# Moving the weight halves by 64 bytes in the on-chip memory of a decoder-trunk kernel

## The reference, cut to what matters

```python
def swiglu(x, wi, wo):
    gt, up = jnp.split(x @ wi, 2, axis=-1)
    return (jax.nn.silu(gt) * up) @ wo

def trunk(x, p, ssm0, conv0, k_hist, v_hist, pos0, hist_valid, w):
    for i in range(DEPTH):
        x = x + 0.5 * swiglu(rmsnorm(x, w['ffn1_norm'][i]), w['ffn1_wi'][i], w['ffn1_wo'][i])
        h = rmsnorm(x, w['mix_norm'][i])
        ...   # mixer (layer 0) or attention (layer 1): out
        x = x + out
        x = x + 0.5 * swiglu(rmsnorm(x, w['ffn2_norm'][i]), w['ffn2_wi'][i], w['ffn2_wo'][i])
        gate = jax.nn.sigmoid(rmsnorm(x, w['ple_norm'][i]) @ w['ple_gate'][i])
        x = x + gate * (p[i] @ w['ple_proj'][i])
```

## The kernel before, in words

| operand | first tile | step from tile to tile | tiles begin at |
|---|---|---|---|
| xh, xl | 128 | 32 | 128, 160, 192, 224, 0, 32, 64, 96 |
| xh2, xl2 | 64 | 32 | 64, 96, 128, 160, 192, 224, 0, 32 |
| hh, hl | 128 | 32 | 128, 160, 192, 224, 0, 32, 64, 96, then again |
| views of wide | 16 | 0 | always 16 |

## Time and profile before

### The profile page before, as it was taken

How to read it: one execution, slowest core, us unless ns; L and a number is a source line. 1 busy time by engine, 2 the same in 40 slices (tenths; PEclk the granted TensorE clock), 3 DMA queues, 4 the chain that set the end, 5 groups by cost and what they waited for, 6 DMA issues and landing times.

```text
span 1182.9 us, 26670 instructions
## 1 busy us (share of the span) xinstructions
PE 1171.8 (99%) x9823; PEld 1150.3 (97%) x9823; DVE 867.8 (73%) x1378; ACT 699.3 (59%) x1150; POOL 248.1 (21%) x354
## 2 busy tenths in 40 slices
PE   9999999999999999999999999999999999999998
PEld 9999999999999899999999999999999899999998
DVE  8667646999899868787645987888468777677448
ACT  6454435777786647555546765555368765544345
POOL 1000002412222202232344233232036310000001
PEclk9999999999999999999999999999999999999999
DMA  8765554755445375876886677657743346555552
GB/s 311 239 205 187 178 180 142 265 186 206 144 168 194 110 227 195 303 233 246 283 307 209 225 272 277 221 175 245 249 155 98 107 158 214 179 181 189 178 183 86
DMA packets 63345, 239.90 MB, mean 203 GB/s; under 512 B 7716, under 2 KB 9680, under 8 KB 58896
## 3 DMA queue, kind: packets, MB, share of 16 engines
q1 hardware_dynamic: 56880, 197.83, 50.1%
q0 software_dynamic: 6112, 40.66, 9.5%
q10 hardware_dynamic: 288, 0.54, 0.1%
HBM read 226.87 MB, written 13.39 MB: 203 GB/s over the span
## 4 chain that ended last, share of the span: by engine, by line
PE 85%; DVE 8%; ACT 3%; issue 2%; DMA 1%; POOL 1%; SPq 0%; DVEq 0%; POOLq 0%; ACTq 0%
PE bank L520 27%; PE bank L521 27%; PE bank L522 27%; DVE wlo L1596 2%; ACT whi L1111 1%; DVE xact L1871 1%; DVE xl L1615 1%; DMA raw<-weights 1%; PE bank L894 1%; DMA x<-xT 0%; POOL sq L2227 0%; DVE x L1626 0%; PE bank L920 0%; PE bank L899 0%; ACT under L1513 0%
## 5 line engine op out<-in xcount | busy, mean ns | idle before, releaser
L1596 DVE TENSOR_TENSOR wlo<-raw,whi 128x1024 fp32r<-128x1024 f32 x367 | 457.9, 1251 | 240.1 <-ACT whi L1111 239.7
L1111 ACT ACTIVATE whi<-raw 128x1024 fp32r<-128x1024 f32 x367 | 385.4, 1054 | 238.0 <-PE bank L522 216.0
L520 PE MATMUL bank<-xh,whi 128*128 128x264 f32 x1304 | 376.0, 288 | 1.1 <-DVE zs L1643 0.9
L521 PE MATMUL bank<-xl,whi 128*128 128x264 f32 x1304 | 370.1, 284 | 0.0
L522 PE MATMUL bank<-xh,wlo 128*128 128x264 f32 x1304 | 369.9, 284 | 0.0
L520 PE MATMUL bank<-wide,whi 128*128 128x264 f32 (+1 forms) x1056 | 299.6, 284 | 0.8 <-DVE wide L1801 0.5
L521 PE MATMUL bank<-wide,whi 128*128 128x264 f32 (+1 forms) x1056 | 298.7, 283 | 0.0
L522 PE MATMUL bank<-wide,wlo 128*128 128x264 f32 (+1 forms) x1056 | 298.3, 282 | 0.0
L520 PEld LDWEIGHTS bank<-xh,whi 128*128 128x128 f32 x1304 | 245.9, 189 | 3.6 <-DVE wlo L1596 1.8
L521 PEld LDWEIGHTS bank<-xl,whi 128*128 128x128 f32 x1304 | 246.1, 189 | 0.8
L522 PEld LDWEIGHTS bank<-xh,wlo 128*128 128x128 f32 x1304 | 244.7, 188 | 0.0
(11 more groups left out here) (345 smaller groups left out, 1250.3 us busy)
## 6 DMA issues: line engine op xcount, KB each, us to landing
raw<-weights SPq DMA_DIRECT2D x367, 512.0 KB, 3.6
under<-ssm POOLq DMA_DIRECT2D x8, 1024.0 KB, 7.5
xact<-ssm POOLq DMA_DIRECT2D x8, 1024.0 KB, 7.2
out_ssm_s<-xact POOLq DMA_DIRECT2D x8, 1024.0 KB, 5.7
xact<-dtx_rows POOLq DMA_DIRECT2D x5, 1024.0 KB, 10.1
zs<-dtx_rows POOLq DMA_DIRECT2D x2, 1024.0 KB, 14.8
x<-xT SPq DMA_DIRECT2D x4, 264.0 KB, 5.1
out_y<-x SPq DMA_DIRECT2D x8, 132.0 KB, 1.7
```

Source lines behind the costliest of these rows:

```text
L520: pe.matmul(out, whi[:, w, c], rh, start=start, stop=False)
L521: pe.matmul(out, whi[:, w, c], rl, start=False, stop=False)
L1111: act.activation(whi[:, s, :], raw[:, s, :], ACT.Copy).then_inc(hi_ready, 1)
L1596: dve.tensor_tensor(wlo[:, s, :], raw[:, s, :], whi[:, s, :].bitcast(F32), ALU.subtract).then_inc(lo_ready, 1)
```

## The change

Two tiles that nothing uses are allocated around the halves of the weights: 16 fp32 values (64 bytes per partition) before `whi`, and 48 (192 bytes) behind `wlo`. `whi` and `wlo` then begin at 192 modulo 256. Together the two are 256 bytes, so all tiles behind them lie 256 bytes further and keep their addresses modulo 256. No instruction is added, removed or moved.

```diff
         raw = sb("raw", [P, RING, UNIT])
+        sb("ahead_w", [P, 16])
         whi = sb("whi", [P, RING, UNIT], F32R)
         wlo = sb("wlo", [P, RING, UNIT], F32R)
+        sb("behind_w", [P, 48])
         x = sb("x", [P, KT, N])
```

## The result

The changed kernel takes 1187.47 us, the median of nine runs (1186.73 to 1189.17); the kernel before takes 1183.99 us in nine runs beside it. The ratio is 1.003, 95% interval 1.0021 to 1.0040: slower by 3.5 us. The profiled execution took 1189.17 us, with a span of 1187.4 us; lines behind L189 are two further down in its trace.

What follows compares the result with a forecast made beforehand. It took TensorE's matmul spacing as the bound. All terms were 0 except -0.19 us on `hh`, half counted: 1184.72 to 1184.6, less 0.51 for the median, 1184.1 us; likeliest range 1182.7 to 1185.5, overall 1178.3 to 1194.8.

Steps and rivals of the forecast that it cites:

- What bounds the kernel: Whole kernel: it is as long as TensorE's matmuls are apart; units on `wide`, `xh` and `hh` make 1051.3 of 1182.9 us.
- VectorE, ScalarE, DMA at nothing: Making the halves: new addresses cost L1596 and L1111 nothing, DMAs write only `raw`; 0 us, at most 1.4 either way.
- xh by the circle, 0: `xh` and `xh2` stages: each unit walks through all eight distances, a shift only starts elsewhere; 163 units x 0.
- hh two units later: `hh` stages: if distance matters, unit k takes the time of unit k - 2; sum -0.19 us.
- wide at 2.880: `wide` stages, 132 units: distance goes from 144 to 80, each unit still takes 2.880 us; 0, at worst +10.6 us.
- The reading between neighbours: `wide` at distance 80: neighbours 64 and 96 take 2.91 us, which would be +4.0 us; rejected because it fails at 144.
- rival 1: `wide` stages: distance 80 is bad, each matmul waits on a clash; +4.0 us, 1188.1, up to 1194.8; chance 0.36.
- The rule on two independent read ports: TensorE: loading the next weights takes no read bandwidth from the running matmul, so distance can't matter; change worth 0.

Runs made afterwards that it cites:

- e11: Kernel before, no address changed, the eight tiles of the `unit_a` units that don't wait for single tiles used in reverse order, 7 to 0: 1186.24 us, ratio 1.0016.
- e14: Kernel before, no address changed, tiles of the same `unit_a` units used in the order 0, 2, 4, 6, 1, 3, 5, 7: 1185.47 us, ratio 1.0008.
- e3: Kernel before, weights left at 128, views of `wide` 64 bytes earlier, so that their distance to the weights is 80: 1187.95 us, ratio 1.0032.
- e2: Changed kernel, weights at 192, views of `wide` 64 bytes further, so that their distance is 144 again: 1184.16 us, ratio 0.9997.
- e5: Kernel before, hidden activations on `wide` in f1o0 and f2o1 with a tile step of 1296 bytes in place of 1280: 1184.98 us, ratio 1.0006.
- e6: Kernel before, both weight halves at 144 by an offset inside their tensors, views of `wide` 16 bytes further (distance still 144): 1185.08 us, ratio 1.0015.
- e9: Kernel before, distance on `wide` held at 128 in f1i0 and f2i1, at 192 in f1o0 and f2o1: 1190.56 us, ratio 1.0053.
- e4: Kernel before with only the high half of the weights moved, `whi` at 192 and `wlo` at 128: 1190.77 us, ratio 1.0054.
- e7: As e4, and on `wide` the high activations begin at 80, the low ones stay at 16: 1185.04 us, ratio 1.0007 against the kernel before.
- e8: Kernel before, hidden activations on `wide` in f1o0 and f2o1 with a tile step of 1284 bytes: 1186.82 us, ratio 1.0025.

## Why the prediction was wrong

1. **What bounds the kernel: right.** The time is the sum of TensorE's start-to-start times; 3.57 us of the difference stand in the two stretches on `wide`.
2. **VectorE, ScalarE, DMA at nothing: right.** L1596 and L1111 keep their means within 1 ns and their medians of 1225 and 1059 ns.
3. **xh by the circle, 0: right,** 26.10 us in both stages, for the reason given. That the sum is the same doesn't mean that a unit's time is a function of its distance: e11 to e14 have the same circle in other orders and other sums. The circle held because the shift kept the order too.
4. **hh two units later: right to the unit, the sum only in part.** The shifted units gained 0.18 us together in the traces, against 0.19. But the sum left out the last two units of each stage, which are done together: they went from 5.83 to 5.86 us in f2o0 and f1o1 and from 5.81 to 5.83 in "sout" and "o", which gives back 0.10 us. That is far below what a measurement tells.
5. **wide at 2.880: the step that failed.** It said "80 isn't one either. I take 2.880, hence 0". The runs show 2.909 us at the distance 80 in the changed kernel and in e3, in all four stages, and 2.880 at 144 in e2: +3.8 us. One good value off the multiples of 32 was taken for a property of all such values. e5 shows units at odd multiples of 16 between 2.88 and 2.92 us. The reading between neighbours, which was written down as rival 1 at +4.0 us and 1188.1 us, came to 2.91 against 2.909. Its agreement is luck as far as the runs show: it fails at 144, and at 128 the `hh` units say 2.96 while a constant distance of 128 runs at 2.880 or 2.960. Behind the failed step stands a premise that the prediction took for granted, that a unit's time is a function of its distance; e6, e9 and e11 to e14 show that it isn't.
6. **The rule on two independent read ports.** Cited beside the forecast: by the Trainium skill, "TensorE: Matmul & The Clock Gate", section "Step-by-step: what each phase is for", loading the next weights takes nothing from the running matmul. The runs differ: with the same instructions, the distance to the weights being loaded moves the pace from 2.880 to 2.909 us (before and after), and from e4 to e7 it goes from 2.933 to 2.880 us when the high activations alone begin 64 bytes further, so that each streaming tile is 144 from the weights loaded meanwhile. The measurement decides.

Rival 1 came true in place and price, and in that the distance decides (0.36 of the chances, against 0.40 for no change); the clash that it names is not shown. The evidence for its own point, that 2.880 is the shortest of all units seen, should have outweighed a single sample.

Open is what clashes inside: why some distances settle at one pace and others at two, and what picks the pace and changes it on the way (e6, e9). No run here measures single reads. Whether 144 or 80 could also show a second pace in some execution can't be excluded; the runs of the kernel before, e2 and e3 show none.

## What to carry to other kernels

Where TensorE is the bound and each matmul brings its own weight load, look at where the moving tile begins relative to the weights that are being loaded. In this kernel it was worth 1% of a matmul's time from one steady distance to another (2.880 to 2.909 us per 24), up to 4% between two paces of one distance (2.880 to 2.987), and up to 5% off multiples of 16 bytes (3.03). A padding changes it for every stage that streams against the tiles it moves, so read the start-to-start times of each stage before and after, not the busy times. A pace that is the shortest seen has, as far as the trace tells, one way to go; keep that distance when tiles move, and repeat the runs, since some distances have two paces.

## What the runs showed of the hardware that was not expected

- The same addresses ran at two steady paces within one execution: 2.880 and 2.960 us per unit (e9), 2.880 and 2.987 (e6). In f1i0 both executions went from the slower pace to the faster one across a break in the stream of matmuls, behind unit 2.
- With the halves of the weights at different addresses one matmul in three took 126 to 127 ns and the others 120 (e4, `wide`).
- 2.880 us, 120.0 ns per matmul of 264 columns, is the shortest steady pace of `xh`, `wide` or `hh` units in any trace here, reached at distances 128, 144 and 192.
- Moving tiles that begin 4 or 8 bytes past a multiple of 16 cost up to 0.15 us per unit, those 12 bytes past it no more than the multiples themselves (2.88 to 2.90 us against 2.88 to 2.92, e8).
- High and low halves at different addresses made `hh` units faster (2.898 against 2.918 us) and `xh` and `wide` units slower (2.907 and 2.933 against 2.900 and 2.880), in e4.
